# A router product with its operands swapped, and the down weights of two expert tiles loaded earlier

## The reference, cut to what matters

```python
def hierarchical_moe(h, wg, bg, we, be, w_gate, w_up, w_down):   # h = rmsnorm(x, norm_moe_g)
    g_logits = (hf @ wg).astype(jnp.float32) + bg                # 4 groups
    ...                                                          # e_logits = hf @ we + be: 16 experts
    combine = ...                                                # best group, then its best 2 of 4 experts
    a = jnp.einsum("nd,edf->nef", hf, w_gate)                    # 16 experts, 1024 -> 256
    b = jnp.einsum("nd,edf->nef", hf, w_up)
    u = jax.nn.silu(a) * b * combine[..., None]
    y = jnp.einsum("nef,efd->nd", u, w_down)                     # 256 -> 1024
```

## Time and profile before

| | |
|---|---|
| median of 3 runs | 1451.93 us (1445.11 to 1454.81) |
| the profiled execution | 1444.45 us, of which the span from the first to the last instruction is 1442.6 us |
| instructions | 19589 |
| TensorE busy | 95% of the span |
| mean granted TensorE clock | 0.974 of full speed |
| DVE, ACT, POOL busy | 50%, 42%, 33% |

### The profile page before, as it was taken

One profiled execution on the slowest core, in us unless ns is written; L12 is line 12 of the kernel. 1 busy time (PEld: TensorE's weight loads), 2 busy tenths in 40 slices (PEclk: granted clock), 3 DMA queues, 4 the chain that ended last, 5 costly groups with the idle time before them and its releaser, 6 DMA issues.

```text
span 1442.6 us, 19589 instructions
## 1 busy us (share of the span) xinstructions
PE 1369.3 (95%) x7922; PEld 1101.0 (76%) x7922; DVE 717.6 (50%) x1064; ACT 608.1 (42%) x957; POOL 478.9 (33%) x182
## 2 busy tenths in 40 slices
PE   6999999998999999999989999999999997899996
PEld 5787877776788888888868887787888876577662
DVE  3276386654445515234051696535245165666655
ACT  4444354454534314223143234744335453365643
POOL 2441132002256636545415463521334510300002
PEclk9999999899999999999998999999999998799998
DMA  6221213201444444445433333211332606899955
GB/s 228 88 95 45 67 58 108 78 2 45 145 152 156 132 145 161 132 142 165 131 123 101 113 102 117 60 59 59 117 134 94 214 1 261 340 403 421 410 234 190
DMA packets 99533, 210.21 MB, mean 146 GB/s; under 512 B 6865, under 2 KB 56401, under 8 KB 92785
## 3 DMA queue, kind: packets, MB, share of 16 engines
q1 hardware_dynamic: 92384, 183.23, 37.1%
q10 hardware_dynamic: 4320, 15.73, 2.7%
q0 software_dynamic: 2736, 9.96, 1.9%
HBM read 171.16 MB, written 37.75 MB: 145 GB/s over the span
## 4 chain that ended last, share of the span: by engine, by line
PE 86%; DVE 5%; issue 3%; DMA 3%; ACT 2%; POOL 1%; SPq 0%; POOLq 0%; DVEq 0%; ACTq 0%
PE bank L529 23%; PE bank L511 14%; PE bank L513 13%; PE bank L512 13%; PE bank L3052 4%; PE bank L875 3%; PE bank L849 2%; PE bank L864 2%; PE bank L762 1%; PE bank L1292 1%; PE bank L2985 1%; PE bank L1269 1%; ACT whi L440 1%; POOL wlo L448 1%; PE bank L3018 1%
## 5 line engine op out<-in xcount | busy, mean ns | idle before, releaser
L448 POOL TENSOR_TENSOR wlo<-raw,whi 128x2048 fp32r<-128x2048 f32 (+1 forms) x82 | 374.1, 4563 | 501.1 <-ACT whi L440 452.4
L440 ACT ACTIVATE whi<-raw 128x2048 fp32r<-128x2048 f32 (+1 forms) x84 | 159.1, 1895 | 254.7 <-PE bank L513 231.9
L2169 DVE TENSOR_TENSOR ffn_relu<-ffn_relu 128x512 f32<-128x512 f32 x32 | 97.7, 3052 | 102.2 <-ACT ffn_relu L2149 102.2
L529 PE MATMUL bank<-alo,whi 128*128 128x512 f32 x352 | 139.9, 398 | 1.5 <-DVE alo L785 1.5
L529 PE MATMUL bank<-ahi,whi 128*128 128x512 f32 x352 | 138.0, 392 | 0.0
L511 PE MATMUL bank<-alo,whi 128*128 128x512 f32 (+1 forms) x344 | 136.9, 398 | 0.0
L513 PE MATMUL bank<-ahi,wlo 128*128 128x512 f32 (+1 forms) x344 | 134.7, 392 | 0.6 <-issue 0.6
L512 PE MATMUL bank<-ahi,whi 128*128 128x512 f32 (+1 forms) x344 | 134.5, 391 | 0.0
L529 PE MATMUL bank<-ahi,wlo 128*128 128x512 f32 x352 | 87.8, 391 | 0.0
L529 PEld LDWEIGHTS bank<-alo,whi 128*128 128x128 f32 x352 | 66.8, 190 | 18.3 <-DVE alo L785 1.9
L529 PEld LDWEIGHTS bank<-ahi,whi 128*128 128x128 f32 x352 | 66.7, 189 | 14.1 <-issue 0.5
(11 more groups left out here) (544 smaller groups left out, 2922.2 us busy)
## 6 DMA issues: line engine op xcount, KB each, us to landing
raw<-in_w_in_dram SPq DMA_DIRECT2D x18, 1024.0 KB, 5.3
expert_gate_up<-in_expert_w_gate_dram SPq DMA_DIRECT2D x17, 1024.0 KB, 10.4
expert_gate_up<-in_expert_w_up_dram SPq DMA_DIRECT2D x17, 1024.0 KB, 13.5
expert_down<-in_expert_w_down_dram SPq DMA_DIRECT2D x17, 1024.0 KB, 8.1
raw<-in_w_ffn_up_dram SPq DMA_DIRECT2D x16, 1024.0 KB, 6.1
raw<-in_w_ffn_down_dram SPq DMA_DIRECT2D x16, 1024.0 KB, 5.6
raw<-in_w_in_first_dram SPq DMA_DIRECT2D x12, 1024.0 KB, 5.4
expert_rows_dram<-zero_rows SPq DMA_DIRECT2D x23, 512.0 KB, 6.9
```

The costliest lines, as they stand in the source:

```text
L440: nc.scalar.activation(whi[:, n % SPLIT, 0:k * c], raw[:, n % RAW, 0:k * c], ACT.Copy).then_inc(hi_made, 1)
L448: nc.gpsimd.tensor_tensor(wlo[:, n % SPLIT, 0:k * c], raw[:, n % RAW, 0:k * c], whi[:, n % SPLIT, 0:k * c].bitcast(F32), ALU.subtract).the ...
L529: ins = nc.tensor.matmul(acc, of, by, start=first and i == 0, stop=last and i == products - 1)
L2169: nc.vector.tensor_tensor(relu2[:, n % 2, :], relu[:, n % 2, :], relu[:, n % 2, :], ALU.mult).then_inc(up_sq, 1)
```

## The change

The router's product has its operands swapped: the weights (20 columns) are stationary and 128 token columns of `h_cols` move, so the sums come out as 20 partitions x 128 tokens. VectorE copies them from PSUM to a new tile `routed`, TensorE transposes that back to 128 x 20, and VectorE adds the bias as before. Each token tile uses two banks in place of one; the bank of the ranks moves with this, and one of the banks of the token lists is another. The down weights of expert tiles 0 and 1 are issued as soon as all slabs have been split (`lo_made`), ahead of the gate and up weights of tile 1.

```diff
@@ router_units
-                banks.plan(f"logits/{t}", (logits_made, t + 1))
-                yield from range(2)
+                banks.plan(f"routed/{t}", (logits_made, 2 * t + 1))
+                yield
+                banks.plan(f"logits/{t}", (logits_made, 2 * t + 2))
+                yield
@@ pe_router
+                ts = slice(t * P, (t + 1) * P)
+                acc = banks.open(pe, f"routed/{t}")
+                for k in range(KD):
+                    ins = nc.tensor.matmul(acc[0:NG + NE, 0:P], router_w[:, k, :], h_t[:, k, ts], start=k == 0, stop=k == KD - 1)
+                banks.filled(ins, f"routed/{t}")
+                yield
+                pe.wait_ge(logits_made, 2 * t + 1)
                 acc = banks.open(pe, f"logits/{t}")
-                for k in range(KD):
-                    ins = nc.tensor.matmul(acc[:, 0:NG + NE], h_t[:, k, t * P:(t + 1) * P], router_w[:, k, :],
-                                           start=k == 0, stop=k == KD - 1)
-                banks.filled(ins, f"logits/{t}")
-                yield from range(2)
+                banks.filled(nc.tensor.transpose(acc[:, 0:NG + NE], routed[0:NG + NE, ts], ident[0:NG + NE, 0:NG + NE]), f"logits/{t}")
+                yield
@@ dve_router
                 yield from range(2)
+                acc = banks.take(dve, f"routed/{t}")
+                nc.vector.tensor_copy(routed[0:NG + NE, t * P:(t + 1) * P], acc[0:NG + NE, 0:P]).then_inc(logits_made, 1)
+                yield
                 acc = banks.take(dve, f"logits/{t}")
                 if t == 0:
                     dve.wait_ge(router_in, 80)
                 nc.vector.tensor_tensor(logits[:, t, :], acc[:, 0:NG + NE], router_b[:, :], ALU.add).then_inc(logits_made, 1)
-                yield from range(2)
+                yield
@@ tiles of phase 5
+        routed = sb("routed", [P, T], at=put.at[0])
         rows = put("expert_rows", [P, 2, D])
...
-        LIST_BANKS = (Y_BANKS[0], Y_BANKS[1], HIDDEN_BANKS[1])
+        LIST_BANKS = (Y_BANKS[0], GATE_UP_BANKS[1], HIDDEN_BANKS[1])
@@ dve_route
-            dve.wait_ge(logits_made, NT)
+            dve.wait_ge(logits_made, 2 * NT)
@@ sp_phase5
+            sp.wait_ge(lo_made, len(slabs))
+            for i in range(2):
+                sp_down(sp, i, i)
             sp.wait_ge(heads_out, attns["xa"]["out"] + XH // attns["xa"]["group"] * NT)
             sp_gate_up(sp, 1, 1)
...
-            for i in range(WEIGHTS):
+            for i in range(2, WEIGHTS):
                 sp_down(sp, i, i)
```

## The result

| | median | runs |
|---|---|---|
| before | 1446.83 us (1441.84 to 1454.85) | 17 |
| with the change | 1456.34 us (1449.2 to 1462.43) | 17 |

The ratio is 1.0052, with a 95% interval of 1.0036 to 1.0069: +5 to +10 us. The profiled execution took 1456.27 us, its span is 1454.5 us. The range of the prediction holds the time, but its likeliest case (+0.2 us) was wrong. The time also falls on that of the slower rival (1456 us); both are partly luck, since the forecast counted from a median of three runs, 1451.93 us, and the 17 runs of before have 1446.83.

The account below looks back on a forecast made before the run. TensorE was taken as the bound behind a hole at the router's waits and gather. +4.4 us (later logits) and -4.2 (shorter gather) gave +0.2 on the median 1451.93: 1452.1 us, range for 8 in 10 1446 to 1459 us.

Parts of the forecast that it names:

- likeliest case: Whole kernel: later logits and a shorter gather nearly cancel, +0.2 us, 1452.1 us against the median; chance 0.55.
- slower rival: At the third tile's stall and the gather: stall stays, gather still takes 7.2 to 8.5 us; +3.1 to +5.4, 1456 us; chance 0.25.
- The product costs nothing more and nothing less: Router product on TensorE: 16 passes a tile at 0.11 us each as before, 0.0 us; bounds 1.7 us either way.
- The hidden round trips of tiles 0 and 1: Router, tiles 0 and 1: cross attention products hide VectorE's copy, one more TensorE pass each remains; +0.3 us in all.
- The third tile's copy behind the split and the second round trip: Router, last two token tiles: copy waits for VectorE's split, then an unhidden round trip; logits 4.4 us later, bounds 1.0 to 5.5.
- The gather from 8.5 to 4.3 us: Gather of expert tile 0's rows: early down loads leave the DMA idle, so it lands in 4.3 us; -4.2 us.
- Tile 0 itself: Expert tile 0: rows land at 1236.8 instead of 1236.6, TensorE goes on as before, clock back after about 5.5 us.
- The scatters: Scatters and ScalarE's load waiting for them: 4.4 us later, absorbed by 3.4 us of slack; 0 to 1 us, taken as 0.
- Idle time of TensorE between tiles 1 and 4: Expert tiles 1 to 4: a sign, listed without a size, that would make the forecast wrong.
- The faster rival: Router, fourth token tile: swapped product runs at full clock; -2.1 us, 1449.8 us; chance 0.15.
- That the stall isn't there: Third token tile's copy: VectorE's split comes earlier or the copy gets ahead of it; -3.2 us, 1448.7 us; chance 0.05.
- Within 1%: Whole kernel: time differs from before by less than 1% (14.5 us); chance 0.94, faster 0.02, slower 0.04.

Follow-up runs that it names:

- after_gate4_waits: The changed kernel plus one wait: SyncE issues tile 4's gate and up weights only when all scatters have landed; 1447.67 us, ratio to before 1.0010.
- swap_only: The changed kernel with only the router's part: all four down loads issued where they were before; 1455.56 us, ratio to before 1.0045.
- after_split_later: The changed kernel with VectorE's split of tile 1's weights issued behind the third tile's copy and addition; ratio to before 1.0025, repeated 1.0039.
- before_gate4_waits: The kernel before plus one wait: tile 4's gate and up weights issued only when all scatters have landed; ratio to before 1.0009.

## Why the prediction was right and wrong, step by step

With the collision taken away (after_gate4_waits) the stretch is 253.5 us against 253.3: the +0.2 that the likeliest case had. The collision is the rest, 263.2 - 253.5 = 9.7 us. That the 0.2 is met so exactly is partly luck, as the terms show.

- **The product costs nothing more and nothing less**: nearly. Its 16 passes take 1193.18 - 1191.33 = 1.85 us, before 1191.04 - 1189.33 = 1.71. The weight load did get shorter, 100 ns for 20 columns (shortest, median and longest in the row)

```profile
L2741 PEld LDWEIGHTS bank<-h_cols,router_w x64: 96/100/157, 1191.3 to 1223.0; 128*20 128x20 f32 x64
```

  against 192 for 128 before. The Trainium skill ("TensorE: Matmul & The Clock Gate", what happens when you issue a matmul) says that a load's time scales with its column count; the trace agrees in the direction, but 100 of 192 ns is about half, where the columns are a sixth. The pass didn't get shorter with the load (1.85/16 = 0.116 us, before 0.107 to 0.113), so in the new pass something other than the load sets the time; that it is the moving side, as I took from the rows of L875, was not tested.
- **The hidden round trips of tiles 0 and 1, +0.3 us**: too small. From the first product to the third it is 20.12 us instead of 19.11, so +1.0; each transpose adds about 0.36 us of TensorE's time, not the 0.11 to 0.2 of my term, and the passes add 0.14 at the first tile and 0.04 at the second.
- **The third tile's copy behind the split and the second round trip, +4.4 us**: right. Without the 0.3 of tiles 0 and 1 it is 4.1, and the rows give 4.0 from the third product; after_split_later shows the split as the cause of the stall.
- **The gather from 8.5 to 4.3 us**: right in size (4.80), wrong in its cause. I gave it to the early down loads and 2.1 MB of freed transfers. swap_only shows 4.84 without them: a gather that is issued 4 us later meets only the bulk's end, and that costs it nothing to speak of. So -4.2 was never a gain of the loads in this kernel, though with the old router they are worth 3.2. The two terms weren't independent, and I added them as if they were.
- **Tile 0 itself, taken as unchanged**: it got shorter. From its first transpose to that of tile 1 it is 1249.84 - 1239.82 = 10.02 us, before 1247.47 - 1236.61 = 10.86, since the clock rose to 2.4 GHz 4.3 us behind tile 0's start and not 6.0 (the granted clock is 0.51 until 1244.2 and 1.00 from there to 1250; before, the rise is at about 1242.6). This 0.8 hides most of the 1.0 of the hidden round trips, and it was not in the sum.
- **The scatters, 0 to 1 us, taken as 0**: this is the step that failed. I moved the last scatter by 4.4 us with its old duration of 8.3 and let ScalarE's slack of 3.4 us absorb it. I named the edge (landed 1253.65, asked for at 1253.70) but held the duration fixed. What decides it is the order of two issues: tile 4's weights came 2.3 us behind the last scatter before, and 2.2 us ahead of it now. The trace of before and the forecast's own shifts give the turn: weights at 1247.66 + 0.2 = 1247.9, last scatter at 1245.35 + 4.4 = 1249.75. The scatter took 11.75 us, the load behind it 8.73, and with the stalls and the clock's fall the price was 9.7 us of the stretch, which after_gate4_waits takes away; before_gate4_waits shows that the wait is worth nothing where nothing collides. Idle time of TensorE between tiles 1 and 4 stood among the signs that would make me wrong, and it is the one that came.
- **The rivals.** The slower rival (1456 us) has the measured time, but its mechanism, a gather that doesn't shrink, is refuted, and its +3.1 to +5.4 us is less than the 9.5 between the medians: it meets the time because it was counted from 1451.93. There I also read the 97.6% of the earlier trace rows as against queues served in turn. In these 2 us GpSimd's queue moved no packet at all, so they say nothing of turns. The faster rival, the clock, was seen in one of three profiles with the split moved, none with the stall. That the stall isn't there was excluded by the lists, and was so.
- **Within 1%**: right. The range of 1446 to 1459 us held the time with the help of its start: counted from the 1446.83 of 17 runs the same range would end at 1453.9.

What stays open: which part of the 9.7 us is the clock's. The fall at 1271.4 comes behind the stalls, and no run has them alone at the same length. The moved split alone reached 252.7 in one profile and 259.3 in the next, with the same lists. In the first, tile 4's weights went out 0.8 us ahead of the last scatter, TensorE idled 2.3 us in tiles 2 and 3 and the clock stayed full; in the second it was 2.3 us ahead, TensorE idled 5.4 us and the clock fell. The fourth product's clock differed too, and how much each did wasn't separated. So an early issue doesn't fix the price: the last scatter took 11.0 to 12.4 us in all six profiles with it, while TensorE idled 2.0 to 6.4 us.

## What to carry to other kernels

When a change moves one transfer against others, write down for each transfer that something waits for what is issued within a few us on either side, and check whether the order of two issues turns over; a duration read from a trace holds only for the company that the transfer had there. Gains of two parts that keep a transfer out of the same traffic don't add: ask of each what the other does to it alone. And before giving a wait to an engine that runs its list in order, look at what stands in front of the instruction that ends the wait, here 2.3 us of unrelated work on VectorE.

## What the runs showed of the hardware

A scatter of GpSimd's slows down in the company of SyncE's large loads. The same scatter of 128 rows of 4 KB took 5.8 to 6.6 us behind the other scatters with SyncE's queue silent (the five profiles with the wait), 8.3 with 2 MB issued 2.3 us after it, and 11.0 to 12.4 with 2 MB issued 0.8 to 2.3 us ahead of it. From after_gate4_waits (5.9) to the change (11.75) it is 5.9 us more; an estimate of what 2.1 MB take at the 424 GB/s of the earlier trace rows is 5.0. The gather took 8.5 and 8.7 us where SyncE's queue stayed full for 4 us behind its issue (before, before_gate4_waits), 4.8 to 5.0 in nine profiles, and 5.7 in after_split_later.

By time and bytes the shares of the two queues are uneven: from 1254 to 1260 us SyncE's had 74.3% and GpSimd's 26.0%. Counted in packets they aren't, once both have some all the time. From 1256 to 1260 us:

```profile
q1 hardware_dynamic: 156, 1.15, 68.3%
q0 software_dynamic: 150, 0.55, 33.8%
```

SyncE's packets carried 7.4 KB each, GpSimd's 3.7, so equal turns gave GpSimd's queue a third of the bytes. The Trainium skill ("DMA: Bandwidth & Descriptors", SWDGE vs HWDGE vs iDMA) has a DMA engine serve its queues in turn; with 156 packets to 150 the trace agrees.
